# Three weight units in step with the splits, a second pair-weight buffer, and products of ones in a one-core decoder layer

## The reference

```
x += 0.5 * post(SwiGLU_1(pre(x)))
h  = pre(x); P = h @ w_in          # columns for both branches, 44 units of 128
y_A = sigmoid(o) * headnorm(mLSTM(q_A, k_A, v_A, i, f))     # 4 heads
y_B = MLA(c_q, c_kv, k_rope)       # 8 heads, paged latent cache for the requests
x += post((sigmoid(g_A) * y_A + sigmoid(g_B) * y_B) @ w_out)
x += 0.5 * post(SwiGLU_2(pre(x)))
```

## Time and profile before

| | before |
|---|---|
| median of three runs | 1492.91 us |
| the profiled execution | 1492.75 us |
| its span in the trace | 1491.0 us |
| mean granted TensorE clock | 0.972 |
| TensorE products busy | 1394.5 us (94%) |
| DVE / ACT / POOL busy | 664.3 / 459.7 / 144.7 us |
| HBM traffic | 115 GB/s over the span |

### The profile page before, as it was taken

One profiled execution on the slowest core, in us unless ns is written; L12 is line 12 of the kernel. 1 busy time (PEld: TensorE's weight loads), 2 busy tenths in 40 slices (PEclk: granted clock), 3 DMA queues, 4 the chain that ended last, 5 costly groups with the idle time before them and its releaser, 6 DMA issues.

```text
span 1491.0 us, 30438 instructions
## 1 busy us (share of the span) xinstructions
PE 1394.5 (94%) x12105; PEld 1310.9 (88%) x12105; DVE 664.3 (45%) x1162; ACT 459.7 (31%) x787; POOL 144.7 (10%) x275
## 2 busy tenths in 40 slices
PE   5999999999967899999999999979789999999995
PEld 5999999999956888887889887759689999999994
DVE  4444444422274445444453555563644444442224
ACT  5222222322243234443342332133432222222221
POOL 0000000000001203554551000000000000000000
PEclk9999999999998999999999999979999999999998
DMA  3222222322215636776676133324122222232221
GB/s 132 85 86 96 86 84 89 106 94 79 85 58 183 197 108 178 230 226 194 203 222 222 43 114 129 116 72 145 43 71 90 93 84 86 97 101 88 88 78 60
DMA packets 79040, 173.05 MB, mean 116 GB/s; under 512 B 12057, under 2 KB 44826, under 8 KB 77530
## 3 DMA queue, kind: packets, MB, share of 16 engines
q1 hardware_dynamic: 70746, 154.87, 31.6%
q0 software_dynamic: 8192, 16.79, 3.9%
HBM read 157.55 MB, written 14.07 MB: 115 GB/s over the span
## 4 chain that ended last, share of the span: by engine, by line
PE 90%; DVE 5%; DMA 2%; ACT 1%; issue 1%; SPq 0%; ACTq 0%; DVEq 0%
PE acc L594 55%; PE acc L701 17%; PE bank_a L799 1%; PE bank_a L770 1%; PE bank_v L814 1%; PE acc L618 1%; PE bank_a L800 1%; PE bank_v L966 1%; PE acc L836 1%; PE acc L868 1%; PE acc L840 1%; PE bank_v L994 1%; PE bank_a L660 1%; DVE tmp L1520 1%; DMA wp<-in_w_pair 1%
## 5 line engine op out<-in xcount | busy, mean ns | idle before, releaser
L1499 DVE TENSOR_TENSOR w_lo<-w_raw,w_hi 128x1024 fp32r<-128x1024 f32 (+1 forms) x172 | 223.5, 1299 | 230.0 <-ACT w_hi L1079 226.3
L594 PE MATMUL acc<-x_hi,w_hi 128*128 128x272 f32 x1472 | 306.6, 290 | 11.1 <-DVE w_lo L1499 11.1
L594 PE MATMUL acc<-x_hi,w_lo 128*128 128x272 f32 x1472 | 304.6, 289 | 0.0
L594 PE MATMUL acc<-x_lo,w_hi 128*128 128x272 f32 x1472 | 304.5, 289 | 0.0
L1079 ACT ACTIVATE w_hi<-w_raw 128x1024 fp32r<-128x1024 f32 (+1 forms) x172 | 191.0, 1110 | 167.9 <-PE acc L594 81.8
L594 PEld LDWEIGHTS acc<-x_hi,w_hi 128*128 128x128 f32 x1472 | 231.6, 190 | 11.9 <-DVE w_lo L1499 11.9
L594 PEld LDWEIGHTS acc<-x_lo,w_hi 128*128 128x128 f32 x1472 | 232.5, 190 | 0.0
L594 PEld LDWEIGHTS acc<-x_hi,w_lo 128*128 128x128 f32 x1472 | 231.2, 190 | 0.0
L701 PE MATMUL acc<-x_hi,w_hi 128*128 128x272 f32 x672 | 207.3, 308 | 10.6 <-DVE w_lo L1499 10.6
L701 PE MATMUL acc<-x_lo,w_hi 128*128 128x272 f32 x672 | 199.7, 297 | 0.0
L701 PE MATMUL acc<-x_hi,w_lo 128*128 128x272 f32 x672 | 199.6, 297 | 0.0
(11 more groups left out here) (269 smaller groups left out, 1351.9 us busy)
## 6 DMA issues: line engine op xcount, KB each, us to landing
w_raw<-in_w_gu SPq DMA_DIRECT2D x88, 512.0 KB, 3.4
pg<-in_key_t SPq DMA_DIRECT2D x256, 96.0 KB, 2.5
w_raw<-in_w_dn SPq DMA_DIRECT2D x32, 704.0 KB, 4.1
w_raw<-in_w_in SPq DMA_DIRECT2D x44, 512.0 KB, 4.5
pg<-in_lat POOLq DMA_DIRECT2D x256, 64.0 KB, 2.7
g_mid<-sq SPq DMA_DIRECT2D x16, 272.0 KB, 3.4
st<-in_c SPq DMA_DIRECT2D x4, 1028.0 KB, 4.9
out_sC<-st SPq DMA_DIRECT2D x4, 1028.0 KB, 3.9
```

The lines of the kernel that those rows point to most:

```text
L594: ins = nc.tensor.matmul(acc[pair][:, a, 0:HT], w[:, slot, n * P:(n + 1) * P], v[:, k, a * HT:(a + 1) * HT], start=first and n == 0 and te ...
L1499: nc.vector.tensor_tensor(wlo[:, slot, 0:tiles * P], raw[:, slot, 0:tiles * P], f32(whi[:, slot, 0:tiles * P]), ALU.subtract).then_inc(w_s ...
```

## The change

- **Three units.** `first_three` takes the place of `first_pair`. Unit 1 is split into two buffers of its own, `w3_hi` and `w3_lo`, laid over `sg` and `gt`; unit 2 goes into slot 1. A third accumulator `acc[2]` is made of the two banks of `bank_v`. For each x tile units 0, 1 and 2 are multiplied; in gu1 the first four tiles of unit 2 are made up after its split. In the last tile unit 2 comes first, then the sum of squares, then units 0 and 1.
- **Raw copy.** DVE copies unit 2's sums unscaled to `tmp` (`take_raw`), which frees its accumulator and, in slot 1, unit 3's split.
- **Order of loads.** Stage in: five units first, then constants and pair weights, then the spill. In gu1 unit 2 is loaded between the halves of x.
- **Products of ones** before the first x_lo: 36 in gu1, 20 in in and gu2.
- **Pair weights** alternate between `wp` and `wp_odd`; the load runs two pairs ahead.
- **Moved on DVE:** the four clears go behind the evictions of the first three units of stage in; `sample_finish(0)` goes before the six feed products.

```diff
+        w3hi, w3lo = at("w3_hi", [P, KD * P], SG_AT, F32R), at("w3_lo", [P, KD * P], GT_AT, F32R)
+        wp_odd = at("wp_odd", [P, 1024], cursor[0])
-        acc = [ctx.enter_context(nc.psum_tensor(f"acc{i}", [P, 2, 512], F32)) for i in range(2)]
+        acc = [ctx.enter_context(nc.psum_tensor(f"acc{i}", [P, 2, 512], F32)) for i in range(3)]
-        V = Ring([ctx.enter_context(nc.psum_tensor(f"bank_v{i}", [P, 512], F32)) for i in range(2)])
+        V = Ring([acc[2][:, i, :] for i in range(2)])
...
                     for j in range(4):
                         sp.dma_start(x[:, 2 * j:2 * j + 2, :], xT[:, 2 * j:2 * j + 2, :]).then_inc(x_landed[j], 16)
-                    weight_units(name, 2, 2)
+                        if j == 1:
+                            weight_units(name, 2, 1)
+                    sp.wait_ge(w_split, 2)
+                    sp.dma_start(raw[:, 1, 0:KD * P], w_gu1[3]).then_inc(w_landed[1], 16)
...
-                sp.wait_ge(a_ready, A.filled(f"qls{p}"))
-                sp.dma_start(wp[:], w_pair[(p + 1) % 4]).then_inc(pair_landed, 16)
+                if p < 3:
+                    sp.wait_ge(a_ready, A.filled(f"qls{p}"))
+                    sp.dma_start((wp_odd if p % 2 else wp)[:], w_pair[(p + 2) % 4]).then_inc(pair_landed[p % 2], 16)
...
+            def first_three(name, norm, x_at, alone=0):
+
+                U, G = STAGE[name][0], STAGE[name][3]
+                w_of = ((whi[:, 0, :], wlo[:, 0, :]), (w3hi[:], w3lo[:]), (whi[:, 1, :], wlo[:, 1, :]))
+                pair_of = (1, 2, 0) if name == "in" else (0, 2, 1)
...
+                if name == "gu2":
+                    pe.wait_ge(v_read, V.n)
+                for _ in range(36 if name == "gu1" else 20):
+                    nc.tensor.matmul(acc[2][:, 0, 0:P], ones[:], ones[:], start=True, stop=True)
                 pe.wait_ge(w_split, U + 2)
                 if G >= 2:
                     pe.wait_ge(acc_read, G)
+                if not alone:
+                    pe.wait_ge(w_split, U + 3)
+                for k in range(KD - 1):
                     pe.wait_ge(x_split, x_at + k + 1)
+                    for j in range(3 if k >= alone else 2):
+                        step(j, k)
+                    if k == alone - 1:
+                        pe.wait_ge(w_split, U + 3)
+                        for k_ in range(alone):
+                            step(2, k_)
+                pe.wait_ge(x_split, x_at + KD)
+                step(2, KD - 1)
+                sum_squares(norm)
+                step(0, KD - 1)
+                step(1, KD - 1)
...
+            def take_raw(name, n):
+
+                dve.wait_ge(w_used, STAGE[name][0] + 1)
+                nc.vector.tensor_copy(halves(tmp[:]), acc[0 if name == "in" else 1][:, :, 0:HT]).then_inc(raw_read, 1)
+                lo_of_first(name, 3)
+                dve.wait_ge(raw_read, n)
...
+                        if norm == "f1pre" and m == 4:
+                            lo_of_first("gu1", 2)
...
                 sample_highest(m)
-                dense(6)
                 if m:
                     sample_finish(0)
-                dense(12)
+                dense(18)
```

More of the change, by code:

```diff
@@ L440, in in_feed @@
             def in_feed():
-                for i in range(2, IN_N):
+                for i in range(3, IN_N):
                     for n in range(UNIT_MM):
@@ L456, in dense @@
                     next(feed, None)
[L458 to L461 removed]
+            for i in range(5):
+                in_unit(i)
             sp.wait_ge(w_used, IN_U)
@@ L630, in body @@
                         start = isinstance(i, int) and i == 0
-                        if start and j == 0 and norm:
-                            first_pair(u0, g0, x_at)
-                            sum_squares(norm)
-                        if not (start and j < 2 and norm):
-                            unit(4 * i + (u0 + j), j % 2, 4 * i + (g0 + j), j % 2, xhi, xlo, range(KD), True, True,
-                                 x_split if start and j == 0 else None, x_at)
+                        if start and norm and j < 3:
+                            if j == 0:
+                                first_three(name, norm, x_at, 4 if name == "gu1" else 0)
+                            continue
+                        if start and norm:
+                            pe.wait_ge(raw_read, 1 if name == "gu1" else 3)
+                        unit(4 * i + (u0 + j), j % 2, 0 if start and norm else 4 * i + (g0 + j), j % 2, xhi, xlo,
+                             range(KD), True, True, x_split if start and j == 0 else None, x_at)
                 if n // 4 > 2:
@@ L1087, in next_unit @@
                         return
-                    tiles = STAGE[ORDER[ORDER.index(name) + 1]][2]
-                if isinstance(i, int) and i == 0 and j == 0 and name in ("gu1", "gu2"):
-                    return
+                    follower = ORDER[ORDER.index(name) + 1]
+                    tiles = STAGE[follower][2]
                 U = first + j + 1
@@ L1137, in body @@
                             act.wait_ge(acc_read, i * 4 + (g0 + j + 1))
-                            nc.scalar.activation(sg[:, 0, :], gt[:, 0, :], ACT.Silu).then_inc(g_act, 1)
+                            nc.scalar.activation(sg[:, 0, :], tmp[:] if first and j else gt[:, 0, :], ACT.Silu)\
+                                .then_inc(g_act, 1)
                         else:
@@ L1168, in _ @@
             act.wait_ge(setup, 1)
-            for U in range(2):
-                hi_part(U, U, KD)
+            hi_part(0, 0, KD)
+            hi_of_first("gu1", 1)
             act.wait_ge(vecs_landed, 16)
@@ L1506, in next_unit @@
                         return
-                    tiles = STAGE[ORDER[ORDER.index(name) + 1]][2]
-                if isinstance(i, int) and i == 0 and j == 0 and name in ("gu1", "gu2"):
-                    return
+                    follower = ORDER[ORDER.index(name) + 1]
+                    tiles = STAGE[follower][2]
                 lo_part(i * 4 + (first + j + 1), (first + j + 1) % 2, tiles)
+                if follower in ("in", "gu2"):
+                    lo_of_first(follower, 1)
             def norm_in(norm, gain, xhi_at, fresh):
@@ L1599, in _ @@
             link(nc.vector.tensor_scalar(vhalf[:, 8:16], vecs[:, V_F2POST:V_F2POST + 8], 0.5, None, ALU.mult))
-            for U in range(2):
-                lo_part(U, U, KD)
+            lo_part(0, 0, KD)
+            lo_of_first("gu1", 1)
             norm_in("f1pre", V_F1PRE, 0, None)
```

151 lines of the change are left out of this document (96 added, 55 removed).

## The result

The changed kernel takes **1443.34 us** in the median of 4 runs (1442.23 to 1444.47), the old one 1492.69 in 4 runs: ratio **0.9671, 95% interval 0.9654 to 0.9687**, 49.4 us less. I had forecast 1447.3 with 1441 to 1455. The profiled execution took 1443.54, its span is 1441.9 (1491.0 before).

A forecast was written before the change was run, and what follows sets the result against it. TensorE carries 90% of the chain, so its idle or half-clock stretches at stage starts and in the pair loop count. Gains 8.4 + 13.8 + 9.6 + 1.5 + 12.3 = 45.6 us give a median of 1447.3, range 1441 to 1455.

The forecast's parts named there:

- Start of gu1: First stage: products of ones, then three interleaved units, let unit 3 start at 31.55 against 40.0; gain 8.4 us.
- T: Time when first_three has issued unit 2's last product; TensorE can start unit 3 at T + 2.65; in gu1 28.9.
- Start of "in": Stage "in": unit 3 starts 17.85 us earlier, less a new 2.3 wait before the fifth unit and 1.7 of clock; gain 13.8.
- the clock keeps up: Stage "in": no clock fall through the new 2.3 us gap; a quarter of the 0.74 forecast case, giving 1445.6.
- Pair weights: Pair loop: the second buffer removes three waits, about 4.2 us, and three clock losses of 1.8 each; gain 9.6 us.
- sample_new: Sampling step: DVE copies the finished output before the unit's eviction and split; ACT's probT copy late next by 0.9; gain 1.5.
- Start of gu2: Stage gu2: unit 3 starts at 1082.4 against 1094.7, and unit 4 waits for nothing; gain 12.3 us.
- Ones that harm: Rival: TensorE stays at 1.2 GHz through the products of ones, gu1 starts 7.5 us later; 1457; chance 0.08.
- Unhidden third unit: Rival: DVE and ACT set unit 4 everywhere, 4 us each in gu1 and gu2 too; 1455; chance 0.08.
- awaited pair loads: Rival, pair loop: page loads fill the queue, half the gain, 4.8 us, is lost; 1452; chance 0.07.
- lagging pages: Rival, attention: each of 16 steps waits for latent pages; 3.2 us per step ends at 1498; chance 0.02.
- a change without effect: Rival: unit 2's DMA is late each time, TensorE waits as before; 1490; chance 0.01.

The follow-up runs named there:

- e7: Changed kernel with the third unit of "in" not interleaved tile by tile, its first seven tiles behind the seventh tile of the other two; 1449.03 us.
- e5: Changed kernel with the loads of the fourth and fifth weight unit of "in" issued behind the x spill, constants and pair weights; 1456.07 us.
- e2: Changed kernel with the old kernel's single buffer for pair weights; 1457.25 us.
- e6: Changed kernel with ACT's rounding of gu2's third unit behind the inverse root and DVE's subtraction behind the first x tile; 1444.69 us.
- e11: Changed kernel without the 20 products of ones of "in", those of gu1 and gu2 kept; 1443.80 us.
- e1: Changed kernel without any products of ones (36 in gu1, 20 each in "in" and gu2); 1442.86 us.
- e3: Changed kernel with the first group's sample_finish behind six fill products in sample_new, as in the old kernel; 1449.26 us.
- e9: Changed kernel run again with nothing edited; 1445.33 us, ratio 0.9682 to the old kernel.

## Why the prediction was right, and where it was off

- **Start of gu1**, 9.2 for 8.4. The ones end at 11.57, not 12.4: they take 0.145 us a record over the slow start (10.42 for 72) and 0.116 in the later series (4.63 for 40), where the earlier trace rows had given 0.13. The order behind them came as worked out: T at 28.0 (28.9), unit 3 at 30.73 (31.55), 2.7 behind T (2.65). The term was sized by the wrong row.
- **Start of "in"**, 14.1 for 13.8. The gap of 2.3 was 2.00, the clock's 1.7 was 1.7. That the third unit hides in the idle time is shown by e7 (4.4 us lost without), that the order of the loads had made the wait by e5 (11.7). The 1.7 was one draw: behind this wait the first run, e2, e6, e7 and e11 lost it, e1, e3 and e9 nothing, three of eight where I had given a quarter to "the clock keeps up". That the first trace had the fall is luck.
- **Pair weights**, 9.6 for 9.6. The mechanism is right (e2: waits and falls both come back). The size is that of the old execution that was profiled, from which I took it; in e2 the single buffer cost 13.0. No page load slowed the passes.
- **sample_new**, 3.3 for 1.5. The step that failed is "TensorE waited 2.37 for it": I priced the wait (1.5, and 1.8 of it went) and left out the fall behind it, some 1.5 us (e3), though the pair loop had shown one behind a wait of 1.26. The next wait is ACT's, as said, 0.58 for 0.9.
- **Last head and "out"**, 1.9 where I had no term. The change edits nothing there. The old run lost 8.5 us to the clock between 968 and 1007, the new one 5.1, and other traces without ones there 5.1 to 11.9, which put the end of this stretch up to 3.2 us later than in the first changed trace. It is luck of the profiled execution.
- **Start of gu2**, 11.0 for 12.3. I moved the x_lo chain unchanged; but ACT waits for the third unit's load ahead of the root, and where that load takes 4.8 us the chain starts 1.1 us later behind the sums (7.58 for 6.49). e6 shows that the order on ACT and DVE cannot win it back; a quicker load does (e11). The step that failed is the one I did not write for gu2: that the load of the third unit lands before ACT wants it. Unit 4 waited for nothing, as forecast.
- **The rivals.** Ones that harm: no, full clock was reached under them, and in e1 their lack costs 1.1 in gu1. Unhidden third unit, awaited pair loads, lagging pages and a change without effect: none showed. The sum was 3.5 short of the trace: 0.8, 0.3, 1.8 and 1.9 too little, 1.3 too much. The 1.9 has no cause in the change, and the errors partly cancel, so the sum came closer than its terms deserve.

## What to carry to other kernels

Price a wait of TensorE of over a microsecond at its length plus a possible fall of the clock behind it, here 0, 1.7 or 3.4 us, and keep both ends in the range: the removed waits of the pair loop were worth over twice their own length. Compare such edits by medians of several runs on one chip, and find the place in the trace by matching the n-th instruction of a regular kind, since one profiled execution can come out up to 3 us later at a place that nobody touched. Work that must be done anyway (a third unit's products, memsets) belongs into idle time that a slower engine's chain leaves; dummy products paid 1.1 us at the start of the program and nothing where the next engine's chain set the pace.
